# Expert weights of a two-layer mixture of experts: a ring of 8 places becomes one of 12, with 15 places at the start of the second layer

## The reference

```python
for l in range(DEPTH):                      # DEPTH = 2
    ...                                     # attention of this layer, added to x (and ctx in the first)
    # layer 0: tokens = ctx and x together, 512 of them; layer 1: x alone, 256
    f = hier_moe(tokens, w_group[l], b_group[l], w_expert[l], b_expert[l], w1[l], w3[l], w2[l])
    x = x + gt2 * f                         # and ctx with its own gate in layer 0
```

## Time and profile before

| | |
|---|---|
| Median of 3 runs | 2405.37 us |
| The profiled execution, its own time | 2406.56 us |
| Its span in the trace | 2404.8 us |
| TensorE clock granted, mean | 0.976 |
| TensorE busy | 2198.2 us (91%) |
| VectorE busy | 946.3 us (39%) |
| DMA, mean | 251 GB/s |
| Expert stage of layer 0 (first to last product) | about 379 to 866 us |
| Expert stage of layer 1 | about 1153 to 1632 us |
| Loads `ring<-in_w` and `rows<-in_w` of the experts | 288 + 96, each 1024 KB |

### The profile page before, as it was taken

How to read it: one execution, slowest core, us unless ns; L and a number is a source line. 1 busy time by engine, 2 the same in 40 slices (tenths; PEclk the granted TensorE clock), 3 DMA queues, 4 the chain that set the end, 5 groups by cost and what they waited for, 6 DMA issues and landing times.

```text
span 2404.8 us, 25890 instructions
## 1 busy us (share of the span) xinstructions
PE 2198.2 (91%) x9488; PEld 1110.9 (46%) x9488; DVE 946.3 (39%) x1780; ACT 351.7 (15%) x939; POOL 163.8 (7%) x208
## 2 busy tenths in 40 slices
PE   6989988999999989988888888889899999999998
PEld 2336553333333334454333333334658744577843
DVE  3567432333333366363222222224550344571245
ACT  1016121000000011051100000001431000251000
POOL 1110002000000002121200000000000000000000
PEclk9999988999999999998999999999999999999999
DMA  9773347999999952204899999994414443504432
GB/s 374 252 277 119 123 166 280 419 419 420 416 421 421 419 220 88 70 1 149 328 421 421 421 421 419 419 419 154 158 58 142 151 170 127 191 7 136 168 147 96
DMA packets 150758, 602.78 MB, mean 251 GB/s; under 512 B 12660, under 2 KB 25716, under 8 KB 101136
## 3 DMA queue, kind: packets, MB, share of 16 engines
q1 hardware_dynamic: 145264, 595.26, 63.1%
q0 software_dynamic: 4736, 5.99, 0.7%
q10 hardware_dynamic: 672, 0.38, 0.1%
HBM read 606.88 MB, written 4.60 MB: 254 GB/s over the span
## 4 chain that ended last, share of the span: by engine, by line
PE 35%; DMA 10%; DVE 5%; issue 1%; ACT 1%; SPq 0%; POOL 0%; DVEq 0%; POOLq 0%; ACTq 0%
PE psum L2841 9%; PE psum L2863 7%; DMA ring<-in_w 5%; PE psum L2680 5%; DMA rows<-in_w 5%; PE psum L2724 4%; PE psum L2312 2%; PE psum L2638 2%; PE psum L2137 2%; PE psum L2649 1%; DVE arena L1733 1%; ACT arena L792 1%; DVE mx L1249 1%; PE psum L2798 1%; DVE X L2014 0%
## 5 line engine op out<-in xcount | busy, mean ns | idle before, releaser
L2638 PE MATMUL psum<-ring,arena 128*64 128x512 f32 x1536 | 349.2, 599 | 43.1 <-DMA ring<-in_w 37.6
L1653 DVE TENSOR_TENSOR arena<-arena,psum 128x512 f32<-128x512 f32 x180 | 123.8, 688 | 295.9 <-PE psum L2649 295.9
L2638 PEld LDWEIGHTS psum<-ring,arena 128*64 128x64 f32 x1536 | 111.9, 137 | 272.8 <-issue 260.0
L2223 PE MATMUL psum<-ring,hT 128*128 128x512 f32 x512 | 229.3, 607 | 2.8 <-DVE hT L1116 1.4
L2841 PE MATMUL psum<-hT,ring 128*128 128x256 f32 x1024 | 221.5, 379 | 2.6 <-DVE hT L1778 2.6
L2841 PEld LDWEIGHTS psum<-hT,ring 128*128 128x128 f32 x1024 | 194.4, 190 | 29.3 <-DVE hT L1778 3.0
L2649 PE MATMUL psum<-arena 128*128 128x512 f32 x384 | 178.6, 601 | 3.0 <-DVE arena L1750 3.0
L2680 PE MATMUL psum<-ring,arena 128*64 128x512 f32 x768 | 171.9, 596 | 1.7 <-DVE arena L1737 1.7
L2137 PE MATMUL psum<-con,arena 128*128 128x128 f32 (+1 forms) x848 | 125.5, 290 | 38.4 <-DVE arena L1733 10.0
L2223 PEld LDWEIGHTS psum<-ring,hT 128*128 128x128 f32 x512 | 98.3, 195 | 122.1 <-issue 119.3
L2137 PEld LDWEIGHTS psum<-con,arena 128*128 128x128 f32 (+1 forms) x848 | 97.8, 146 | 93.1 <-issue 22.7
(11 more groups left out here) (335 smaller groups left out, 2391.2 us busy)
## 6 DMA issues: line engine op xcount, KB each, us to landing
ring<-in_w SPq DMA_DIRECT2D x288, 1024.0 KB, 13.3
rows<-in_w SPq DMA_DIRECT2D x96, 1024.0 KB, 13.6
ring<-in_w_ff SPq DMA_DIRECT2D x64, 1024.0 KB, 5.9
ring<-in_w_mod SPq DMA_DIRECT2D x32, 1024.0 KB, 13.4
ring<-in_w_in_c SPq DMA_DIRECT2D x12, 1024.0 KB, 7.4
gate<-in_w_mod SPq DMA_DIRECT2D x10, 1024.0 KB, 14.4
ring<-in_w_in SPq DMA_DIRECT2D x8, 1024.0 KB, 5.4
ring<-in_w_out SPq DMA_DIRECT2D x8, 1024.0 KB, 6.5
```

The lines of the kernel that those rows point to most:

```text
L1653: dve.tensor_tensor(f, f, bank, ALU.add).then_inc(v_free, 1)
L2223: inst = pe.matmul(bank, hT[:, k, P * m:P * m + P], w[k], start=k == 0, stop=k == KB - 1)
L2638: inst = pe.matmul(out[64 * e:64 * e + 64, :], xgT[:, b, k, 64 * e:64 * e + 64], m, start=k == 0, stop=k == KB - 1)
```

## The change

The ring of the expert stages takes memory that the stage itself does not use at that time. Two new tables (`LEAD_PLACES`, `STEADY_PLACES`) give the places for the first `LEAD_PAIRS` pairs (1 in layer 0, 3 in layer 1) and for the rest. New places are 14 (the upper half of `hT`), 15, 16, 17 and 18 (parts of `arena`); 8 (`gate`) and 12 (`X`) existed. Layer 0 has 12 places all along, layer 1 has 15 in its first three pairs and 12 after them. To make room, the table's derived rows (`slot_token`, `slot_weight`) lie elsewhere and are made before the index is; one of layer 1's gates is loaded later; and ScalarE has one more small instruction, which tells SP that pair 0's tokens have been taken.

```diff
-EXPERT_RING = 8
+LEAD_PLACES = [[0, 1, 2, 3, 4, 5, 6, 7, 8, 14, 16, 15], [0, 1, 2, 3, 4, 5, 12, 17, 18, 8, 6, 7, 14, 16, 15]]
+STEADY_PLACES = [[0, 1, 2, 3, 4, 5, 6, 7, 8, 14, 16, 15], [8, 6, 7, 14, 16, 15, 0, 1, 2, 3, 4, 5]]
+LEAD_PAIRS = [1, 3]
+EXPERT_LAPS = [(PAIRS - 1 - n) // 2 for n in LEAD_PAIRS]
...
+            if i == 14:
+                return hT[:, 4:8, :].rearrange("p a n -> p (a n)")
+            at = {15: 10240, 16: 15360, 17: 6144, 18: 2048}[i]
+            return arena[:, at:at + CHUNK]
...
                 gathered(0)
+                act.activation(mark[:, 1:2], par[:, 0:1], ACT.Copy).then_inc(first_gathered, 1)
...
                     dve.wait_ge(table_in, 16 * l + 16)
+                    for tile in range(nt):
+                        dve.tensor_scalar(slot_token[:, tile, :], slot_tab[:, :, 0], -float(P * tile), None, ALU.add)
+                    dve.tensor_copy(slot_weight[:, 0, :], slot_tab[:, :, 1])
                     dve.tensor_copy(slot_index[:, :], slot_tab[:, :, 0]).then_inc(slots_ready, 1)
                     dve.wait_ge(slots_ready, so_far(slots_ready))
-                    for tile in range(nt):
-                        dve.tensor_scalar(slot_token[:, tile, :], slot_tab[:, :, 0], -float(P * tile), None, ALU.add)
-                    dve.tensor_copy(slot_weight[:, 0, :], slot_tab[:, :, 1]).then_inc(v_step, 1)
-                    dve.wait_ge(v_step, so_far(v_step))
...
-                slots.resize(EXPERT_RING)
-                for j in range(EXPERT_RING):
-                    if j == RING:
-                        sp.wait_ge(x_ready, 1 + l)
-                        if l == 0:
-                            gate_load(gate[:, 1], 1, 0, 2)
-                            gate_load(gate[:, 0, 0:1], 0, 1, 1)
-                        else:
-                            gate_load(gate[:, 1, 0:1], 1, 1, 1)
+                slots.places, slots.at = LEAD_PLACES[l], 0
+                for n, place in enumerate(LEAD_PLACES[l]):
+                    if n == RING:
+                        sp.wait_ge(x_ready, 1 + 2 * l)
+                        gate_load(gate[:, 1, 0:nt // 2], 1, l, nt // 2)
+                    if place == 6:
                         sp.wait_ge(ss_ready, 3 + 3 * l)
-                    chunk(0, j)
-                sp.wait_ge(hrow_ready, l + 1)
-                sp.dma_start(h_rows[l].rearrange("(t p) n -> p t n", p=P), hrow[:, 0:nt, :]).then_inc(h_stored, 16)
-                sp.wait_ge(x_scattered, 16 * (8, 12)[l])
-                sp.dma_start(slot_tab, slot_table[l][0:EXPERTS * SLOTS].rearrange("(p e) w -> p e w", e=PAIRS)).then_inc(table_in, 16)
+                    if place == 14:
+                        sp.wait_ge(hrow_ready, l + 1)
+                        sp.dma_start(h_rows[l].rearrange("(t p) n -> p t n", p=P), hrow[:, 0:nt, :]).then_inc(h_stored, 16)
+                        sp.wait_ge(x_turned, PAIRS * l + 1)
+                    if place == 16:
+                        sp.wait_ge(rounds_ready, l + 1)
+                    if place == 15:
+                        sp.wait_ge(x_scattered, 16 * (8, 12)[l])
+                        sp.dma_start(slot_tab, slot_table[l][0:EXPERTS * SLOTS].rearrange("(p e) w -> p e w", e=PAIRS)).then_inc(table_in, 16)
+                        sp.wait_ge(first_gathered, l + 1)
+                        sp.wait_ge(slots_ready, l + 1)
+                    chunk(n // 12, n % 12)
...
             experts(0)
+            sp.wait_ge(used, slots.user[8] + 1)
+            gate_load(gate[:, 0, 0:1], 0, 1, 1)
             matrix(t["w_in_c"][0], 6)
```

More of the change, by code:

```diff
@@ L254, in build @@
         slot_tab = arena[:, 10752:11008].rearrange("p (e w) -> p e w", w=ENTRY)
-        slot_token = arena[:, 11008:11072].rearrange("p (t e) -> p t e", t=4)
-        slot_weight = arena[:, 11072:11088].rearrange("p (t e) -> p t e", t=1)
+        slot_token = arena[:, 17520:17584].rearrange("p (t e) -> p t e", t=4)
+        slot_weight = arena[:, 17584:17600].rearrange("p (t e) -> p t e", t=1)
         x_value = arena[:, 11088:11216].rearrange("p (n w) -> p n w", w=ENTRY)
@@ L321, in build @@
         zeroed = sem("zeroed")
-        loaded = [sem(f"loaded{i}") for i in range(max(MIDDLE_PLACES) + 1)]
+        loaded = [sem(f"loaded{i}") for i in range(max(LEAD_PLACES[1]) + 1)]
         used = sem("used")
@@ L342, in build @@
         h_stored, table_in, slots_ready = sem("h_stored"), sem("table_in"), sem("slots_ready")
+        first_gathered = sem("first_gathered")
         x_fetched = [sem(f"x_fetched{b}") for b in range(2)]
@@ L1727, in pair @@
                     if ends:
-                        dve.wait_ge(gate_in, 48 + 16 * l)
+                        dve.wait_ge(gate_in, 32 + 32 * l)
                         settled(ORDER[l][:nt // 2])
@@ L2693, in moe @@
                 tallies = {v_done: 2 * per_pair, a_done: 4, **{f: 1 for f in fetched}}
-                tallies.update({c: 24 // EXPERT_RING for c in chunk_in[:EXPERT_RING]})
-                slots.resize(EXPERT_RING)
-                pair(0, adds=False)
-                with laps(pe, PAIRS // 2 - 1, tallies):
+                tallies.update({chunk_in[i]: 2 for i in STEADY_PLACES[l]})
+                slots.places, slots.at = LEAD_PLACES[l], 0
+                for n in range(LEAD_PAIRS[l]):
+                    pair(n % 2, adds=n > 0)
+                slots.places, slots.at = STEADY_PLACES[l], 0
+                with laps(pe, EXPERT_LAPS[l], tallies):
                     for b in (1, 0):
@@ L2976, in experts @@
-                sp.wait_ge(hrow_ready, l + 1)
-                sp.dma_start(h_rows[l].rearrange("(t p) n -> p t n", p=P), hrow[:, 0:nt, :]).then_inc(h_stored, 16)
-                sp.wait_ge(x_scattered, 16 * (8, 12)[l])
-                sp.dma_start(slot_tab, slot_table[l][0:EXPERTS * SLOTS].rearrange("(p e) w -> p e w", e=PAIRS)).then_inc(table_in, 16)
-                first, after = slots.count, PAIRS // 2 - 1
+                slots.places, slots.at = LEAD_PLACES[l], 0
+                for n, place in enumerate(LEAD_PLACES[l]):
[3 more added lines that the diff above has]
+                    if place == 6:
+                        sp.wait_ge(ss_ready, 3 + 3 * l)
+                    if place == 14:
[10 more added lines that the diff above has]
+                    chunk(n // 12, n % 12)
@@ L2981, in experts @@
+                for n in range(len(LEAD_PLACES[l]), 12 * LEAD_PAIRS[l]):
+                    chunk(n // 12, n % 12)
+                slots.places, slots.at = STEADY_PLACES[l], 0
+                first, after = slots.count, EXPERT_LAPS[l]
                 with sp.Fori(0, after) as i:
                     freed.laps = [(i, 24)]
-                    for j in range(EXPERT_RING, EXPERT_RING + 24):
-                        chunk(2 * i + j // 12, j % 12)
+                    for j in range(24):
+                        chunk(2 * i + LEAD_PAIRS[l] + j // 12, j % 12)
@@ L2985, in experts @@
                     freed.laps = []
                 slots.count = first + 24 * after
-                slots.user = {s: n + 24 * (after - 1) for s, n in slots.user.items()}
-                for j in range(EXPERT_RING, 24):
-                    chunk(PAIRS - 2 + j // 12, j % 12)
+                slots.user.update({s: slots.user[s] + 24 * (after - 1) for s in STEADY_PLACES[l]})
+                for j in range(12):
+                    chunk(PAIRS - 1, j)
                 slots.resize(RING)
```

4 lines of the change are left out of this document (2 added, 2 removed).

## The result

| | before | after |
|---|---|---|
| Median of the runs | 2405.37 us (2403.73 to 2411.78, 5 runs) | 2391.50 us (2382.46 to 2394.86, 5 runs) |
| Ratio, 95% interval | | 0.9941 [0.9921, 0.9960] |
| Span of the profiled execution | 2404.8 us | 2390.8 us |
| TensorE clock granted, mean | 0.976 | 0.971 |
| TensorE busy | 2198.2 us | 2204.7 us |

What follows compares the result with a forecast made beforehand. The weight stream at 420 GB/s was taken to bound both expert stages. Filling idle time ahead was to save 10.2 us in layer 0 and 13.2 in layer 1: 2405.37 - 23.4 = 2382.0 us, range 2377 to 2390 us.

Steps and rivals of the forecast that it cites:

- the sum: Both expert stages: 10.2 + 13.2 = 23.4 us off, giving 2382.0 us from the median; chance 0.6.
- 4 chunks further: Layer 0: at 385.26 us, when the stream became full before, it is 4 chunks ahead, 4 x 2.54 us.
- the ring's depth: Both expert stages: depth, not stream, sets the pace; all TensorE weight waits go, to about 2342 us; chance 0.03.
- slower places: Both expert stages: new places take weights at 390 GB/s, not 420; 12 us slower, 2417 us; chance 0.05.
- layer 0, 10.2 us: Layer 0's expert stage ends 10.2 us earlier by four chunks loaded ahead; bounds 8.8 and 13.3 us.
- The upper bound of 13.3 us: Layer 0: the most it can give, if all pairs took 29.84 us like the last, which waits for no weight.
- layer 1, 13.2 us: Layer 1's expert stage: stream 6 chunks ahead, restart 2.0 us later, 6 x 2.54 - 2.0; bounds 10 and 15.2 us.
- the price: A weight chunk is worth 2.54 us of stream, from layer 1's pair of 12 chunks in 30.5 us.
- The gather: Pair 1's gather, about 1 us later, costs nothing: lands at 391.5 to 394 us in layer 0, wanted at 395.3.
- 3 us of stall within 3.1 us to spare: Layer 0: were the gather's cover gone, 3 us of stall would fit TensorE's margin over the stream, 13.3 - 10.2 us.
- The first rival: Both layers: scatter, table and gather caught behind the weight stream; gain only 17 to 20 us, about 2387 us; chance 0.22.

Runs made afterwards that it cites:

- experiment 5: Against the changed kernel, the cast making the gather's index goes first again and SP waits for the derived rows by their own signal: 2392.61 us, ratio 0.9948.

## Why the prediction was wrong, point by point

**The steps that failed.** Two terms of the sum were too large, and a third was missing. Layer 0 gave 8.2 us and not 10.2: the stream was not "4 chunks further" at its restart but three. Layer 1 gave 11.3 us and not 13.2: its six chunks were worth 2.35 us each and not 2.54, and the restart moved by some 2.7 us and not 2.0. That makes 19.5 us in place of 23.4. The rest, down to the 13.9 us of the first runs, is a difference between executions, which the sum put at nothing without saying so; it may hold a loss of 2 to 3 us in the second block, which stays open.

**Right: what bounds the kernel, and what the change takes away.** Share 1.01 and 421 GB/s in both stages, so the rivals of the ring's depth and of slower places fall. TensorE's waits for weights were to be about 35 us and are 35.7. The next stage's weights after layer 0 stayed hidden: its first product comes behind the same wait of 1.4 us for VectorE as before.

**Mis-sized: layer 0, 10.2 us.** The step that failed is "at the moment at which the stream became full before, it is 4 chunks further". That moment was read from one execution as 385.26 us. It is set by TensorE's first release in the expert stage, and in this execution TensorE had a stretch of the lower clock just ahead, 0.78 on average in 371.3 to 386.5 us. The same window in another execution of the same kernel:

```profile
371.30:386.50 15.20, 14.45 (x88) 7.98 (x89) 1.78 (x9) 3.07 (x4) 8.75 (x9) 0.99 0.45 156
```

and its queue:

```profile
379.98 0.33 SPq L2979 DMA_DIRECT2D arena<-slot_table  x1
380.72 4.32 SPq L2936 DMA_DIRECT2D ring<-in_w  x4
```

Of six profiles with eight places in layer 0, four restarted at 380.0 to 381.3 us, with a clock of 0.97 to 1.00 in this window, and two at 385.3 and 386.1, both with 0.78. With twelve places chunk 11 goes at 381.4 us on average of eight profiles (378.6 to 384.5), three chunks after the one that restarts the stream before. Against the usual restart that is three chunks less 0.6 us, 3 x 2.54 - 0.6 = 7.0 us; against the late one 7.6 + 3.9 = 11.5. The last products agree: 854.5 us on average of the four and 859.0 and 859.2 in the two, 847.8 with twelve places, so 6.7 and 11.3 us. The mean of all six is 856.0, a gain of **8.2 us** (plus or minus 2.3). From the restart to the last product it is 473.6 us before and 466.4 after, 7.2 us for three chunks, and the restart is 1.0 us earlier on average. The upper bound of 13.3 us was worked out from the same late execution.

**Mis-sized: layer 1, 13.2 us.** Counted from layer 0's last product, layer 1's came 764.8 us later on average with eight places (six profiles) and 753.5 us with fifteen (seven), a gain of **11.3 us** (plus or minus 1.3). The restart was forecast 299.8 us after layer 0's last product and is at 299.5 (298.6 to 300.6 in five profiles), with one error hidden by another. The scatter held the table up. From its last issue to the table's (1154.81 us before, 1143.24 after), GpSimd's timelines of before and then of after give 2.15 and 4.67 us:

```profile
1152.66 0.96 POOL L537 DMA_INDIRECT slot_table<-arena,x_index  x1 [0.30 <-issue]
```

```profile
1138.57 0.96 POOL L546 DMA_INDIRECT slot_table<-arena,x_index  x1 [0.30 <-issue]
```

It is 2.1 to 2.2 us in six profiles with eight places in layer 1 and 4.6 to 4.8 in seven with fifteen; in layer 0 it grew from 2.1 to between 2.9 and 3.2. The prediction had looked for the delay elsewhere, in the table's read standing behind the weights. But the queue had run dry before that read was issued (DMA share 0.04 and 0.00 in the two us from 1142 on), and it took 2.0 us. In return VectorE's small instructions took less than the 0.2 us each that were allowed for them:

```profile
1145.25 0.26 DVE L1670 TENSOR_SCALAR arena<-arena 128x16 f32<-128x16 f32 x2 [10.52 <-DMA arena<-slot_table]
1145.42 0.17 DVE L1671 COPY arena<-arena 128x16 f32<-128x16 f32 x1
1145.51 0.17 DVE L1672 CAST slot_index<-arena 128x16 int32<-128x16 f32 x1
```

The restart before was at 297.2 us on average, not at the 297.85 of the one execution. So the restart moved by 2.3 us in those five profiles, and by 2.7 on average of all seven with fifteen places.

The larger error is the price. From the restart to the last product it is 467.6 us with eight places (467.3 to 468.0 in six profiles) and 453.5 with fifteen (453.1 to 453.9 in seven): 14.1 us for six chunks, **2.35 us** each, where 6 x 2.54 = 15.2 were forecast. 14.1 - 2.7 = 11.4 agrees with the 11.3 measured. The 2.54 us had a share of the gathers in it, and these run whether a chunk is loaded ahead or not; by the rate alone it is 2.50, so that explains 0.3 of the 1.2 us. The other 0.9 us stays open.

**The gather.** That TensorE would not wait for it in layer 0 was wrong: it waited 4.6 us, though the table came earlier: TensorE reached the transposes at 389.57 - 4.61 = 385 us and not at 395.3, which was again the late execution: in three others of the kernel before TensorE is there at 390.1 to 391.4 us, and waits 1.8 to 2.6 us itself. That it costs nothing was right: the stream still ends the stage (experiment 5). The words on it, 3 us of stall within 3.1 us to spare, rested on the late execution.

**The sum.** 8.2 + 11.3 = 19.5 us in the two stages, where 23.4 were forecast. The cut kernels, which end right behind them, give 19.1. The first rival (17 to 20 us, small transfers behind the stream) has the right size; its mechanism is there with the 2.5 us of the scatter, and explains at most that much, since the restart came where it was forecast. The whole kernels give 16.4 us (plus or minus 2.5) over all executions, and 13.9 was the draw of the first five. In the profiled one 11.2 us were lost in the second block, at a lower granted clock. The mean clock was 0.9728 in those five runs against 0.9747 over all sixteen, 0.0019 x 2390 = 4.5 us; of those five only the profiled one shows that it was lower in the second block. The prediction did not speak of it at all, and treated two executions as if they differed by the change alone. The mean of all sixteen, 2387.9 us, lies in the range given. That would have been luck: the terms would have been too large all the same.

## What to carry to other kernels

Where a stream is full to the end of a stage, time is gained by what is issued before it becomes full: count the chunks ahead of the restart and the shift of the restart, both on the queue's own timeline. Read the instant of a restart from several executions if TensorE's release sets it: here it came 4 to 5 us later where a stretch of lower clock lay just ahead, a fifth of what was to be gained. Price a chunk without what is transferred anyway, and expect somewhat less: 2.2 to 2.5 us here, where the period divided by 12 gave 2.54. And where the gain is below 1%, compare a point in the trace behind the edited stage, or cut the kernel there, before the rest is allowed to add its own scatter.

## What the runs showed of the hardware

- Executions of one and the same kernel differ in where TensorE is granted the lower clock. The second block, from layer 1's last product on, took 780.1 to 786.5 us in three profiles of the kernel before and 780.1 to 791.5 in three of the changed one, with the same matmuls. Time and mean clock go together: 2382.4 us at 0.978, 2394.9 us at 0.970.
- With weights flowing on SP's queue while GpSimd scattered, SP could issue the table's read 2.5 us later (4.67 us after the last scatter's issue, not 2.15). The read itself, issued with the queue dry in both kernels, reached VectorE after 2.0 to 2.1 us.
- Weights land in `gate`, `hT`, `X` and `arena` at the rate of those in `ring` and `rows`: 421 GB/s with the new places, 420 before.
